# Mixture-of-experts stage with 32-row pieces in four column groups, in plain order, with slots refilled by part

## The reference

```python
def _grouped_moe(t, router_w, router_b, w_gate, w_up, w_down):
    scores = jax.nn.sigmoid((t @ router_w).astype(jnp.float32))
    ...
    e_idx = lax.top_k(jnp.where(in_group, sel, -jnp.inf), TOP_K)[1]
    ...
    for e in range(N_EXPERTS):
        he = jax.nn.silu(t @ w_gate[e]) * (t @ w_up[e])
        y = y + gates[:, e:e + 1] * (he @ w_down[e]).astype(jnp.float32)
```

## Time and profile before

| | us |
|---|---|
| median of 3 runs | 1304.79 |
| lowest, highest run | 1302.65, 1305.33 |
| span of the profiled execution, first to last instruction | 1307.4 |
| PE busy in it | 1111.2 (85%) |
| DVE busy | 385.9 (30%) |
| ACT busy | 363.3 (28%) |
| POOL busy | 87.4 (7%) |
| moved by DMA | 317.77 MB, mean 243 GB/s |
| mean granted TensorE clock | 0.913 |

### The profile page before, as it was taken

How to read it: one execution, slowest core, us unless ns; L and a number is a source line. 1 busy time by engine, 2 the same in 40 slices (tenths; PEclk the granted TensorE clock), 3 DMA queues, 4 the chain that set the end, 5 groups by cost and what they waited for, 6 DMA issues and landing times.

```text
span 1307.4 us, 16832 instructions
## 1 busy us (share of the span) xinstructions
PE 1111.2 (85%) x5809; PEld 683.2 (52%) x5810; DVE 385.9 (30%) x1019; ACT 363.3 (28%) x766; POOL 87.4 (7%) x145
## 2 busy tenths in 40 slices
PE   5799999998975599999998479999984987887993
PEld 2244554533435566676754257754672554454652
DVE  1366545555135000000010066655333000000012
ACT  3222345454023111222122152345231322221221
POOL 0000000000001101010001200000001110000111
PEclk9899999998996799999999779989885999988996
DMA  9920495696322269999999960230332899999953
GB/s 320 402 112 1 164 365 197 221 333 229 118 100 87 103 248 384 347 399 350 398 350 398 403 258 1 89 121 1 129 129 81 298 380 382 382 380 388 375 191 113
DMA packets 127534, 317.77 MB, mean 243 GB/s; under 512 B 5872, under 2 KB 6144, under 8 KB 127488
## 3 DMA queue, kind: packets, MB, share of 16 engines
q1 hardware_dynamic: 113680, 276.54, 57.1%
q0 software_dynamic: 12096, 40.38, 8.5%
q10 hardware_dynamic: 1712, 0.23, 0.1%
HBM read 296.68 MB, written 19.40 MB: 242 GB/s over the span
## 4 chain that ended last, share of the span: by engine, by line
PE 66%; SPq 11%; DVE 7%; DMA 7%; ACT 3%; issue 3%; POOL 1%; ACTq 1%; POOLq 0%; DVEq 0%
PE bank L570 17%; SPq L298 11%; PE bank L429 9%; PE bank L597 8%; PE bank L521 7%; PE bank L467 6%; DMA ring<-in_w_up_dram 4%; PE bank L495 3%; PE bank L372 3%; PE bank L478 3%; PE bank L560 2%; PE bank L532 1%; DVE h_t L996 1%; PE bank L438 1%; PE bank L417 1%
## 5 line engine op out<-in xcount | busy, mean ns | idle before, releaser
L570 PE MATMUL bank<-ring,h_t 128*64 128x256 f32 (+1 forms) x2176 | 316.4, 400 | 31.3 <-DMA ring<-in_w_up_dram 28.5
L570 PEld LDWEIGHTS bank<-ring,h_t 128*64 128x64 f32 (+1 forms) x2176 | 231.5, 157 | 104.5 <-issue 44.8
L597 PE MATMUL bank<-ring,h_t 128*64 128x512 f32 (+1 forms) x544 | 151.8, 597 | 17.3 <-DVE h_t L1179 14.6
L429 PE MATMUL bank<-h_t,ring 128*128 128x512 f32 (+1 forms) x320 | 117.5, 522 | 12.3 <-ACT h_t L705 12.3
L1170 DVE COPY h_t<-bank 128x256 f32<-128x256 f32 x52 | 22.1, 424 | 338.0 <-PE bank L570 338.0
L597 PEld LDWEIGHTS bank<-ring,h_t 128*64 128x64 f32 (+1 forms) x544 | 56.5, 149 | 91.2 <-issue 91.2
L429 PEld LDWEIGHTS bank<-h_t,ring 128*128 128x128 f32 x320 | 62.4, 196 | 60.2 <-issue 40.9
L996 DVE TENSOR_REDUCE h_t<-bank 128x1 f32<-128x512 f32 (+1 forms) x96 | 57.7, 601 | 106.3 <-PE bank L467 106.0
L521 PE MATMUL bank<-tokm,ring 128*128 128x512 f32 (+1 forms) x256 | 86.9, 504 | 1.1 <-DVE tokm L1018 1.1
L560 PE MATMUL bank<-cst,h_t 128*128 128x128 f32 x288 | 40.6, 286 | 38.3 <-DMA h_t<-h_rows 38.3
L977 DVE RECIPROCAL work<-work 128x512 f32<-128x512 f32 (+1 forms) x20 | 54.3, 2713 | 58.6 <-ACT work L715 58.6
(11 more groups left out here) (175 smaller groups left out, 1105.6 us busy)
## 6 DMA issues: line engine op xcount, KB each, us to landing
ring<-in_w_gate_dram SPq DMA_DIRECT2D x32, 2048.0 KB, 16.3
ring<-in_w_up_dram SPq DMA_DIRECT2D x32, 2048.0 KB, 22.4
ring<-in_w_down_dram SPq DMA_DIRECT2D x32, 2048.0 KB, 21.9
ring<-in_ada_w_dram SPq DMA_DIRECT2D x24, 2048.0 KB, 8.6
ring<-in_w_in_dram SPq DMA_DIRECT2D x8, 1536.0 KB, 21.8
h_t<-h_rows POOLq DMA_DIRECT2D x18, 512.0 KB, 7.0
ring<-in_w_out_dram SPq DMA_DIRECT2D x4, 2048.0 KB, 7.9
y_rows<-work POOLq DMA_DIRECT2D x52, 128.0 KB, 5.3
```

The source lines that it names most:

```text
L429: last = mm(bank[1 + i % 2][:, 0:widths[i]], qk_weights(i, k), h_t[:, k, 0:widths[i]], start=(k == 0), stop=(k == KD - 1))
L570: last = mm(o, hc_t[:, k, 0:rows], w[s][:, k, 256 * half:256 * half + 256], start=(k == 0), stop=(k == KD - 1))
L597: last = mm(o, he_t[:, k, 0:rows], wd[:, k, 512 * n:512 * n + 512], start=(k == 0), stop=(k == KF - 1))
```

## The change

Both layers get pieces of 32 rows (`CHUNK = 32`, `LEAST = [1, 1]`: at least one piece for an expert). With the counts above layer 0 has 40 pieces and layer 1 has 23. The short and long paths go; so does the table `short`.

- A piece's gate and up product has 32 products of 32 stationary and 256 moving columns, spread over four column groups (gate and up, two halves each), all in bank 1. The down product has 16 such, four column groups for the four quarters of the 1024 output columns, in bank 4.
- A row of 1024 is loaded as four rows of 256 on four partitions (`hc` is 128 x 256), so that 2 transposes turn 32 rows, and one copy by ScalarE, which reorders them, makes `hc_t`. `he` is 128 x 256 and turned by 2 transposes. One Silu, one product with up, one copy to `yrow`, one store.
- The order on TensorE is gate and up, next rows, turn of `he`, down, in `expert_short`, for both layers (the other order, `expert_long`, is in the code and not used with `LEAST = [1, 1]`). ScalarE's order becomes next rows, Silu, result. ScalarE, VectorE and GpSimd have one flat loop in both layers.
- `set_free` and its products go. SP waits for `gu_mm` of an expert's last piece and loads gate and up of expert e + 3, then for `down_mm` and loads down. SP waits for `route_ready` first, since it reads `first`.
- The router's tables grow: `GT` from 26 to 50 entries, so that the operations over `GT` x 16 go from 416 to 800 elements, and the comparison of counts from 48 to 240.

```diff
-SHORT = P // 2
-CHUNK = [P, SHORT]
+CHUNK = 32
+LEAST = [1, 1]
...
+            def refill(l, e, a):
+
+                done = end_of(sp, l, e)
+                sp.wait_ge(gu_mm[l], done)
+                load_expert(l, e + 3, a, (0, 1))
+                sp.wait_ge(down_mm[l], done)
+                load_expert(l, e + 3, a, (2,))
...
-                with sp.Fori(1, 5) as i:
+                sp.wait_ge(route_ready, l + 1)
+                with sp.Fori(0, 4) as i:
                     for a in range(3):
-                        sp.wait_ge(set_free[l][a], i)
-                        load_expert(l, 3 * i + a, a)
-                sp.wait_ge(set_free[l][0], 5)
-                load_expert(l, 15, 0)
+                        refill(l, 3 * i + a, a)
+                refill(l, 12, 0)
...
+                def gate_up(g, a):
+
+                    w = [ring[:, 3 * a + s, :].rearrange("p (k n) -> p k n", k=KD) for s in range(2)]
+                    pe.wait_ge(hc_ready[l], g + 1)
+                    for k in range(KD):
+                        for q in range(4):
+                            last = mm(bank[1][CHUNK * q:CHUNK * q + CHUNK, 0:256], hc_t[:, k, :],
+                                      w[q // 2][:, k, 256 * (q % 2):256 * (q % 2) + 256],
+                                      start=(k == 0), stop=(k == KD - 1))
+                    last.then_inc(gu_mm[l], 1)
...
+                def expert_short(e, a, turns, prev):
+
+
+                    g0, g1 = first_of(pe, l, e), end_of(pe, l, e)
+                    with pe.Fori(g0, g1) as g:
+                        weights_in(a, turns, (0, 1))
+                        gate_up(g, a)
+                        turn_rows(g + 1)
+                        turn_he(g)
+                        weights_in(a, turns, (2,))
+                        down(g, a)
...
+                def rows_turned(n):
                     act.wait_ge(hc_turned[l], n + 1)
...
+                    do(hc_t.rearrange("p (q j) r -> p j q r", j=2),
+                       bank[5][:, 0:256].rearrange("p (j r q) -> p j q r", j=2, q=4), ACT.Identity
+                       ).then_inc(hc_ready[l], 1)
...
+                else:
+                    with act.Fori(0, all_chunks(act, l)) as g:
+                        rows_turned(g + 1)
+                        gated(g)
+                        row_out(g)
...
                 def load_rows(n):
-                    pool.dma_start(hc[0:rows, :], h_rows[bass.ds(row_of(n), rows), :]).then_inc(hc_in[l], 16)
+                    pool.dma_start(hc, h_rows[bass.ds(row_of(n), CHUNK), :].rearrange("r (q c) -> (r q) c", q=4)
+                                   ).then_inc(hc_in[l], 16)
...
+                with dve.Fori(0, all_chunks(dve, l)) as g:
+                    dve.wait_ge(gu_mm[l], g + 1)
+                    v.tensor_copy(he, bank[1][:, 0:256]).then_inc(he_ready[l], 1)
+                    dve.wait_ge(silu_done[l], g + 1)
+                    v.tensor_tensor(he_t, act_g, turned_he[:, :, 2 * CHUNK:P], ALU.mult).then_inc(het_ready[l], 1)
```

More of the change, by code:

```diff
@@ L99, in constants @@
     e = np.arange(NE)
[L100 to L102 removed]
+    t[:, C_TRI:C_W16] = (e[None, :] < np.arange(NE + 1)[:, None]).reshape(-1)
     t[:, C_W16:C_W4] = NE - e
@@ L574, in chunk @@
[L574 to L590 removed]
+                    for j in range(2):
+                        last = turn(bank[5][:, P * j:P * j + P], hc[:, P * j:P * j + P], ident)
@@ L595, in chunk @@
-                        for n in range(2):
-                            o = bank[(4, 7)[n]][:, :] if rows == P else bank[4][rows * n:rows * n + rows, :]
-                            last = mm(o, he_t[:, k, 0:rows], wd[:, k, 512 * n:512 * n + 512],
-                                      start=(k == 0), stop=(k == KF - 1))
-                    last.then_inc(down_mm[l], 1)
-                def expert(e, a, turns):
-                    expert_chunks(pe, l, e, lambda g, rows: chunk(a, turns, g, rows))
-                    mm(bank[0][:, 0:1], ones[:, :], ones[:, 0:1], start=True, stop=True).then_inc(set_free[l][a], 1)
+                        h = he_t[:, k % 2, CHUNK * (k // 2):CHUNK * (k // 2) + CHUNK]
@@ L905, in _, with chunk @@
                 load_rows(1)
-                def chunk(g, rows):
+                def chunk(g):
                     pool.wait_ge(hc_turned[l], g + 2)
@@ L910, in chunk @@
                     pool.wait_ge(rows_ready[l], g + 2)
-                    row = row_of(g)
-                    for s in range(2):
-                        src = yrow[:, 512 * s:512 * s + 512] if rows == P else yrow[rows * s:rows * s + rows, 0:512]
-                        pool.dma_start(y_rows[bass.ds(row, rows), 512 * s:512 * s + 512], src
-                                       ).then_inc(rows_stored[l], 16)
-                chunks(pool, l, chunk)
-                total = pool.value_load(first[0:1, NE:NE + 1], min_val=1, max_val=MAX_CHUNKS[l])
-                pool.wait_ge(rows_stored[l], total * 32 + 16)
+                    pool.dma_start(y_rows[bass.ds(row_of(g), CHUNK), :].rearrange("r (q c) -> q r c", q=4), yrow).then_inc(rows_stored[l], 16)
+                with pool.Fori(0, all_chunks(pool, l)) as g:
+                    chunk(g)
+                total = all_chunks(pool, l)
+                pool.wait_ge(rows_stored[l], total * 16 + 16)
                 pool.wait_ge(hc_in[l], total * 16 + 32)
```

212 lines of the change are left out of this document (83 added, 129 removed).

## The result

The changed kernel takes **1384.46 us** (median; 1379.34 to 1385.18) against 1304.86 of the kernel before on the same chip: 1.0603 times as long, 95% interval 1.0581 to 1.0625. Its profiled execution has a span of 1383.4 us where the one before has 1307.4, 76.0 more.

What follows compares the result with a forecast made beforehand. Chunk length on TensorE bounds layer 0 and layer 1's end, the weights' transfer between. -2.6 + 97.8 - 3.1 - 18.3 + 20.4 = +94.2 on 1307.4, less 2.6 to the median: 1399 us, range 1320 to 1430.

Steps and rivals of the forecast that it cites:

- the likeliest case, with the clock falling: Expert stages: TensorE falls from 2.4 to 1.2 GHz at most pieces, 9.75 us each; 1399 us, chance 0.62.
- register loads: TensorE at an expert's start: 0.05 us a piece on average, most of them under the down product.
- falls of the clock: TensorE's gap before the down product: falls in five pieces of six, 1.7 us each, 1.40 a piece.
- The piece at full clock: Expert stages: product to copy 3.74, gap 2.80, down product to next piece 1.76, together 8.30 us.
- The table load between the next rows and Silu: ScalarE's loop: a load queued after the next rows' copy delays Silu by 1.28 us, making the gap 2.80.
- Layer 1 to expert 12: Weight-bound stretch: earlier first refill, -10.7, and fewer row bytes, -7.6; together -18.3 us, expert 12 starting at 1180.
- The tail: Layer 1, experts 12 to 15: ten pieces of 9.75 plus 1.7, 99.2 us against 78.8, +20.4.
- Between the stages: After layer 0: the last store to `y_rows` lands alone instead of beside `w_in`, -3.1 us.
- At no cost, the row's way out and the store: Row's way out hides under the next gate and up product; the store, 5.4 us to land, is wanted 8 later.
- the second rival: ScalarE's table load is not on Silu's way: gap 1.72, piece 7.27, 1275 us; chance 0.11.
- the third rival: GpSimd's row loads land late: with 7.6 us landing every piece takes 9.2, 1371 us; chance 0.05.
- The signs named in advance: Two table loads a piece, 64 records in 3.7 us, gap 2.8, clock 6 to 8 tenths, expert 12 near 1180.

Runs made afterwards that it cites:

- run 2: Changed kernel plus three useless TensorE products behind the turn of `he`, filling the wait before the down product: 1345.02 us, ratio 1.0309 to the kernel before.
- run 1: Changed kernel with ScalarE's loop taking Silu ahead of the next rows: 1326.23 us, ratio 1.0154 to the kernel before.
- Run 6: On run 5: TensorE's loop over experts unrolled 16 times, each expert's end read one expert ahead: 1304.64 us, ratio 0.9988 to the kernel before.
- Run 3: Changed kernel with each weight slot refilled as a whole after the expert's last down product: 1385.38 us, ratio 1.0627 to the kernel before.
- run 9: On Run 6 plus two result buffers in turn: slots refilled as a whole after the expert's last down product; 1300.77 us, ratio 0.9956 to the kernel before.
- run 5: On run 1: GpSimd reads row numbers into registers ahead of its waits instead of behind them: 1310.39 us, ratio 1.0025 to the kernel before.

## Why the prediction was right, step by step

The forecast was 1399 us and the likeliest case, with the clock falling, is what happened; the time is 14.5 us below it, inside the range. The mechanism was right; how close the number came is in part luck, for two terms of the sum were wrong in opposite directions. Layer 0's stage was forecast at 391.7 us and took 377.6:

| term of layer 0, us | forecast | measured |
|---|---|---|
| 40 pieces at full clock, without register loads | 332.0 | 327.2 |
| register loads | 2.0 | 14 (run 2) |
| slow first product | 1.7 | 1.3 |
| falls of the clock | 56.0 | 34, net (run 2) |

The terms measured are rounded, and 0.8 us of run 2's stage are in none of them.

- **The piece at full clock**, 8.30 forecast: 8.18. The product is 3.73 to VectorE's copy (3.74), the gap 2.74 (2.80), down to the next product 1.72 (1.76). The four column groups stream at half the time of two, as the earlier trace rows said: 64 records take 3.66 where the two groups took 7.13. The loss that the Trainium skill (TensorE: Matmul & The Clock Gate, Part 3) measured with three groups isn't there with these four.
- **The table load between the next rows and Silu**: right in place and size, and run 1 shows it to be the cause of the gap. The Trainium skill (ScalarE: Activation LUTs, "What ACT_TABLE_LOAD costs") has a drain of about 1.38 us beside a load; Silu begins at 453.54, 0.01 after its load, and the load 0.02 after the copy before it. Right also that the gap starts the clock's falls: run 2 keeps gap and load and loses the falls.
- **Falls of the clock**, forecast in five pieces of six at 1.7 each. The price was right: in the changed kernel's layer 0 the products are 47.7 us longer than at full clock (the first one left out), over 28 falls 1.7 each. Two things were over-sized. There were 28 falls, not 33. And of the 47.7 only 34 are net, for under a down product at the low clock nearly all of the register loads are hidden: the 15 changes of expert cost 14.1 us in run 2, and in the changed kernel the spaces from a down product to the next piece are longer by only 1.2 us in all.
- **0.05 a piece for register loads**: too small by a factor of seven. Run 2 shows 14.1 us for 15 changes of expert, 0.35 a piece. Run 6 took them away and gained 6 us; most of the rest turned into waiting.
- **Layer 1 to expert 12**: -22.2 against -18.3, the right sign and near in size. SP issued the first refill at 1088.57, 5.2 us into the stage (forecast: when the slow first product ends), where it was 15.5, 10.3 earlier. Run 3 and run 9 say how much of the 22.2 comes from the part-by-part refill itself: a part, not all. The rest was put down to the shorter first piece and the smaller rows; no run separates these two.
- **The tail**: 16.9 of 20.4, the same over-sized falls (10 pieces of 9.57).
- **Between the stages**: this stretch can't test the -3.1. It is untouched by the experiments and was 260.4 to 272.8 us long in them.
- **From the span to the median**: the sum took 2.6 us off, as in the kernel before. The changed kernel's profiled span, 1383.4, lies 1.1 below its median instead. Span against span the forecast is 18.2 us too high, not 14.5; the other 3.7 are chance.
- **At no cost, the row's way out and the store**: right in the changed kernel (ScalarE waited for GpSimd's stores 11.2 us in all its 63 pieces), and the reason why the second rival would have missed. Had the load not been on the way, the forecast said 1275; run 1 is that case and took 1326. The cover named for the store was the 8 us of a piece, with 5.4 to land. At 7.1 us a piece the store's 7.0 of landing, 0.73 of issue and GpSimd's 1.3 of start are no longer under it, and the landing isn't a constant: 5.7 us (median) in layer 0 of the change at 9.4 us a piece, 6.6 in run 2 at 8.6, 7.0 in run 1 at 8.4. That is the third rival's mechanism, with results late more than rows; it doesn't show in the changed kernel and bounds the faster ones here.
- **The signs named in advance**: two loads a piece, 3.66 for the records and 2.74 for the gap came. Two others were set badly. The clock row reads 8 or 9 in every slice that lies wholly in layer 0's stage, not 6 to 8. And "near 1180" for expert 12 is counted on the old kernel's time, without what layer 0 adds; on the changed kernel's the forecast's own sum gives about 1272, and it began at 1256.81.

## What to carry to other kernels

Read the order of a ScalarE loop for the function sets before its times: a body that begins with a plain copy and then needs Silu loaded two tables per round, the one that begins with Silu loaded one, off the way. When a stage is cut into pieces about as short as a DMA takes to issue and land (7.7 us here), everything that was hidden at the longer period (a store's landing, an issue behind a wait on a shared queue, a register read behind a semaphore) becomes the period in turn; price each step against the **new** piece, not against the old one. Where TensorE must wait a few microseconds in every round, work without use in that wait can be cheaper than the clock it would lose (39 us of 1384 in run 2). Silu first and the filled gap together weren't tried.

## What was not expected of the hardware

- Identity ran behind Silu without a table load of its own: in the expert stages there are 63 loads in run 1, 126 in the change, 32 in the loop of two pieces. A load took 1283 ns each time; on the way to Silu it had 0.02 us of idle before it and 0.01 behind it.
- A store of 128 KB, 1 KB from each of 128 partitions, landed after 5.7 us in layer 0 of the change and after 6.9 in layer 1 (medians), and after 7.0 in layer 0 of run 1, where the pieces follow each other faster. The kernel before had 52 stores of the same 128 KB, 2 KB from each of 64 partitions, which landed after 5.3. Whether the form or the neighbours in time make the difference wasn't tested.
- Issuing a DMA from ScalarE's queue cost it 1.05 us, and the table load behind it began 1.55 after the copy, where it had begun 0.02 after it.
- The clock fell in none of 40 pieces when TensorE's wait of 2.80 us was partly filled (run 2), and 28 times when it was not; even then four pieces running passed at 1.00. In run 5 gaps of 2.60, 2.53 and 3.18 us in three pieces running passed at 1.00, and three others of 2.82 to 3.15 were followed by a fall. What tells them apart the runs don't show.
